# mLSTM denominators: GpSimd adds the scores of the key tiles before the product with ones

## The reference, cut to what matters

```
# per head (4 heads of 128 query/key and 256 value columns), q, k, v over 272 tokens
S    = (q k^T) * exp(D - m_t)          # 272 x 272, causal
num  = S v      + the earlier chunks' part
den  = S.sum(axis=-1) + the earlier chunks' part
h    = num / max(|den|, exp(-m_t))
hm   = rms_norm(h, out_norm_g)
ym   = hm * sigmoid(mo) * silu(mgate)
```

## Time and profile before

| | |
|---|---|
| runs | 1448.88, 1449.24, 1450.42 us |
| profiled execution | 1448.88 us, span 1447.1 us |
| TensorE busy | 1432.7 us (99%) |
| VectorE busy | 1092.7 us (76%) |
| ScalarE busy | 853.7 us (59%) |
| GpSimd busy | 273.1 us (19%) |
| granted clock of TensorE | 0.999 of full speed |

### The profile page before, as it was taken

One profiled execution on the slowest core, in us unless ns is written; L12 is line 12 of the kernel. 1 busy time (PEld: TensorE's weight loads), 2 busy tenths in 40 slices (PEclk: granted clock), 3 DMA queues, 4 the chain that ended last, 5 costly groups with the idle time before them and its releaser, 6 DMA issues.

```text
span 1447.1 us, 27343 instructions
## 1 busy us (share of the span) xinstructions
PE 1432.7 (99%) x9657; PEld 1321.4 (91%) x9657; DVE 1092.7 (76%) x2021; ACT 853.7 (59%) x1559; POOL 273.1 (19%) x329
## 2 busy tenths in 40 slices
PE   8999999999999999999999999999999999999998
PEld 7888899988888888889988888999999999999998
DVE  6777679877756777667787766898778779976883
ACT  6665458766544666446566554656757555576762
POOL 1111113121102111014031113332250035121000
PEclk9999999999999999999999999999999999999999
DMA  6667754556565656565456565554345555434533
GB/s 211 196 196 211 233 180 131 186 179 202 183 188 182 191 187 198 186 195 164 159 171 201 181 188 175 164 145 124 88 127 142 164 153 155 134 94 124 147 118 117
DMA packets 247875, 241.25 MB, mean 167 GB/s; under 512 B 15456, under 2 KB 246736, under 8 KB 247784
## 3 DMA queue, kind: packets, MB, share of 16 engines
q1 hardware_dynamic: 244888, 236.73, 53.8%
q10 hardware_dynamic: 2896, 3.30, 0.8%
HBM read 238.92 MB, written 1.07 MB: 166 GB/s over the span
## 4 chain that ended last, share of the span: by engine, by line
PE 87%; DVE 7%; ACT 3%; issue 2%; DMA 1%; ACTq 0%; SPq 0%; DVEq 0%
PE bank L690 78%; DVE w_lo L1862 2%; DVE work L2458 1%; PE bank L989 1%; ACT w_hi L1124 1%; PE bank L1007 1%; PE bank L972 1%; PE bank L918 1%; DMA raw<-in_w_out_dram 1%; PE bank L928 1%; DVE work L1899 1%; DVE work L2481 1%; DMA raw<-in_ffn_w_in_dram 1%; PE bank L988 1%; ACT L1156 0%
## 5 line engine op out<-in xcount | busy, mean ns | idle before, releaser
L690 PE MATMUL bank<-x_both,w_hi 128*128 128x512 f32 (+2 forms) x3216 | 748.1, 336 | 0.6 <-DVE h L1962 0.5
L1862 DVE TENSOR_TENSOR w_lo<-raw,w_hi 128x1024 fp32r<-128x1024 f32 (+1 forms) x429 | 519.4, 1234 | 203.3 <-ACT w_hi L1124 202.2
L1124 ACT CAST w_hi<-raw 128x1024 fp32r<-128x1024 f32 (+1 forms) x429 | 429.3, 1028 | 125.4 <-PE bank L690 108.3
L690 PEld LDWEIGHTS bank<-x_both,w_hi 128*128 128x128 f32 x3216 | 468.0, 189 | 3.5 <-DVE w_lo L1862 1.1
L690 PEld LDWEIGHTS bank<-x_both,w_lo 128*128 128x128 f32 x2312 | 406.1, 189 | 62.7
L690 PE MATMUL bank<-x_both,w_lo 128*128 128x256 f32 (+1 forms) x2312 | 462.4, 281 | 0.0
L690 PE MATMUL bank<-y_both,w_hi 128*128 128x512 f32 (+2 forms) x1376 | 331.5, 342 | 1.8 <-DVE w_lo L1862 1.1
L690 PEld LDWEIGHTS bank<-y_both,w_lo 128*128 128x128 f32 x1040 | 184.3, 188 | 31.3
L690 PE MATMUL bank<-y_both,w_lo 128*128 128x256 f32 (+1 forms) x1040 | 206.1, 280 | 0.0
L690 PEld LDWEIGHTS bank<-y_both,w_hi 128*128 128x128 f32 x1376 | 200.3, 189 | 2.8 <-DVE w_lo L1862 1.8
L1749 POOL TENSOR_TENSOR work<-work,rstd 128x256 f32<-128x256 f32 x88 | 67.0, 783 | 412.7 <-ACT work L1193 412.7
(11 more groups left out here) (312 smaller groups left out, 1397.9 us busy)
## 6 DMA issues: line engine op xcount, KB each, us to landing
raw<-in_ffn_w_in_dram SPq DMA_DIRECT2D x176, 512.0 KB, 3.8
raw<-in_w_in_dram SPq DMA_DIRECT2D x100, 512.0 KB, 3.7
raw<-in_ffn_w_out_dram SPq DMA_DIRECT2D x64, 512.0 KB, 4.6
raw<-in_w_out_dram SPq DMA_DIRECT2D x32, 512.0 KB, 4.0
raw<-in_ffn_w_out_dram SPq DMA_DIRECT2D x32, 384.0 KB, 3.4
raw<-in_rec_w_in_dram SPq DMA_DIRECT2D x16, 512.0 KB, 4.4
raw<-in_sg_w_in_dram SPq DMA_DIRECT2D x16, 512.0 KB, 4.1
raw<-in_rec_w_out_dram SPq DMA_DIRECT2D x8, 512.0 KB, 3.5
```

Source lines behind the costliest of these rows:

```text
L690: i_ = mm(accs[m][:, cols], w[:, j, m * P:(m + 1) * P], moving, start=begin and g == 0 and not residual, stop=final)
L1124: nc.scalar.copy(hi_part(U)[:, 0:n, :], raw[:, s, 0:n, :]).then_inc(hi_made, 1)
L1862: TT(lo_part(U)[:, 0:n, :], raw[:, s, 0:n, :], hi_part(U)[:, 0:n, :].bitcast(fp32), SUB).then_inc(lo_made, 1)
```

## The change

GpSimd gets a new function, `sums_over_keys`. For each head it adds the second key tile's scores to those of the first in columns 128 to 271, and the third tile's in columns 256 to 271, into `d_sum`, which lies in the place of `v_att`, and raises `d_summed`. TensorE makes the denominators of the queries 0 to 127 from the first tile alone and, after `d_summed`, those of the queries 128 to 271 from `d_sum`.

```
+        d_sum = v_att
...
+        d_summed = sem("d_summed")
...
-                        for t, (a, b) in enumerate(LT):
-                            i_ = mm(bank[4][:, a:L], ones[:, :], m_pt[:, MOFF[t]:MOFF[t] + L - a], start=t == 0, stop=t == 2)
-                        i_.then_inc(m_num, 1)
+                        mm(bank[4][:, 0:P], ones[:, :], m_pt[:, 0:P], start=True, stop=True)
+                        pe.wait_ge(d_summed, n + 1)
+                        mm(bank[4][:, P:L], ones[:, :], d_sum[:, P:L], start=True, stop=True).then_inc(m_num, 1)
...
+                def sums_over_keys():
+
+                    for n in range(M_H * l, M_H * (l + 1)):
+                        pool.wait_ge(m_pt_new, n + 1)
+                        if n % M_H == 0:
+                            pool.wait_ge(kx_mm, l + 1)
+                        else:
+                            pool.wait_ge(m_num, n)
+                        a, b = MOFF[1], MOFF[2]
+                        link(TT(d_sum[:, P:L], m_pt[:, P:L], m_pt[:, a:b], ADD))
+                        TT(d_sum[:, 2 * P:L], d_sum[:, 2 * P:L], m_pt[:, b:MW], ADD).then_inc(d_summed, 1)
+
+                if l:
+                    sums_over_keys()
                 if l == 0:
                     pool.wait_ge(final_r, 1)
                     for c in range(NC8):
                         link(nc.gpsimd.tensor_scalar(h[:, c, META:L], h[:, c, META:L], pcol("final_norm", c), None, MUL))
                         TT(h[:, c, META:L], h[:, c, META:L], sq[:, META:L], MUL).then_inc(h_final, 1)
                     pool.wait_ge(h_final, NC8)
+                    sums_over_keys()
                     h_squares(7, "proj0", 0)
```

## The result

| | before | after |
|---|---|---|
| median | 1449.25 us (18 runs) | 1451.96 us (18 runs) |
| range of the runs | 1448.46 to 1450.42 us | 1449.77 to 1453.96 us |
| profiled execution | 1448.88 us, span 1447.1 | 1453.01 us, span 1451.2 |

The ratio of after to before is 1.0018 (95% interval 1.0012 to 1.0025): 2.7 us slower. The forecast was 1453.2 us. The sign held, and the time lies in the range, but two of the steps that gave it were wrong, and something that I had given 0.06 happened. The median lies 0.1 us under 1452.1 us, where the prediction let slower begin, so by its own bounds the change fell among the outcomes within 0.2%, which had 0.27, and not under slower, which had 0.69. One thing stands out before any trace is opened: the runs after spread over 4.2 us, those before over 2.0.

A forecast was written before the change was run, and what follows sets the result against it. The prediction took the VectorE chain as the bound, with TensorE counting only at head 0 of a layer. To 1448.88 us it added +2.65, +1.05, -0.46 and +1.05, giving 1453.2 us, range 1450.6 to 1455.7 for 8 in 10.

The forecast's parts named there:

- the outcomes within 0.2%: Whole kernel: free additions, no stall at head 0, and the forecast's low end, together 0.27; slower began at 1452.1 us.
- What bounds the kernel: mLSTM: the VectorE chain sets the end, inversions 17.54 us apart; it hangs on TensorE only at head 0 of a layer.
- The wait that is added, layer 0, head 0: TensorE stands 3.0 us for GpSimd's additions, queued behind the final norm; the next unit starts 2.65 us late.
- Layer 1, head 0, denominators shorter: At layer 1's head 0, TensorE's shorter denominators pass their saving to the VectorE chain: -0.46 us.
- What the additions cost VectorE: Heads 1 to 3 of each layer: GpSimd's additions hold VectorE back 0.35 us a head, +1.05 us a layer.
- A small stall there would end ahead of the wait at L1056.: Head 3 of layer 0: additions need 2.1 of 2.4 us; any small stall is covered by an existing wait, costing nothing.
- The clock: Rival: TensorE's clock falls to 1.2 GHz for the unit behind head 0's stall, doubling its 3.09 us: 1456.3 us, chance 0.06.
- The sum: Whole kernel: +2.65, +1.05, -0.46 and +1.05, together +4.3 us on 1448.88, giving 1453.2 us.
- the forecast's own range: Whole kernel, stall and held VectorE: 1451.8 (stall 2.3, 0.15 us a head) to 1455.6 us (3.0, 0.65), chance 0.68.
- What would show it.: Profile signs: 3 us wait at layer 0's head 0, first additions 1.6 us, longer L1056 waits, layer 0 inversions 17.9 us apart.

The follow-up runs named there:

- Two products alone: The kernel before with two denominator products of 128 and 144 columns, no GpSimd additions and no wait for them, denominators incomplete: 1448.25 us, ratio 0.9992.
- the stall filled: The changed kernel with 11 unused products of ones on TensorE ahead of its wait for GpSimd at head 0 of layer 0: 1451.41 us, ratio 1.0018.
- the additions alone: The kernel before, its three products kept, plus GpSimd's additions whose result nobody reads: 1449.10 us, ratio 1.0000.
- the first kernel on GpSimd's kinds: The kernel before with three products plus unread GpSimd instructions, differing by head in size, inputs or operation: 1447.95 us in one run.

## Why the prediction came out, and where its steps failed

- **What bounds the kernel.** Right. The end hangs on the VectorE chain, and only head 0 of a layer passes a change of TensorE on. Two products alone gave 1.1 us less and not 3.7; 3.8 us of waits for GpSimd in later heads cost nothing.
- **"The wait that is added, layer 0, head 0", +2.65 us.** Right. The wait is 2.75 us, the additions 0.49 and 0.22 (taken as 0.50 and 0.25), and with the stall filled the first inversion is later by 2.65.
- **"Layer 1, head 0, denominators shorter", -0.46 us.** Right in kind. From the start of the numerators to the inversion it is 8.67 us where before it was 9.03, so 0.36 of the 0.46 us arrive.
- **"What the additions cost VectorE", 3 x 0.35 us a layer.** Wrong: 0. I took one pair of rows in which GpSimd got in between two splits and carried them to a row of ready VectorE instructions in which it never does. GpSimd lost every turn and paid for it, and I had put the price on VectorE. With the additions alone the ratio is 1.0000. The trace of before has no GpSimd instruction of these kinds that stands longer than 1.9 us, so this row of losses could not be read from it.
- **"A small stall there would end ahead of the wait at L1056."** The place was right, the size was not: with three turns lost and not one, TensorE waits up to 1.25 us at L1054 for GpSimd. As said, it takes the place of the wait at L1056 and costs nothing.
- **The clock.** I had it as a rival with 0.06, because no row that I had read from before has a pause of that length. It fell in all four profiles of the change. The price was too high: I had doubled the whole unit, +3.09 us, and the unit grew by 1.5 us in the first profile; the time grew by 0.6 to 1.2.
- **The sum.** 2.65 for the stall and -0.36 for layer 1 leave +2.3 us, and the stall filled, which is just that, gave +2.1. The forecast added 2.1 us for VectorE, which did not come. The clock put 0.6 to 1.2 us in its place. So 1453.2 is 1.2 us above the median, and what nearness there is comes from a term that was wrong and one that was left out. That 1453.2 lies by the 1453.01 us of the profiled execution is luck twice over, as that one also lost 0.8 us at its start. The bounds of the forecast's own range are misadded: from 1448.88, with the terms given, they come to 1451.6 and 1455.3, not 1451.8 and 1455.6.
- **"What would show it."** The wait of about 3 us came as 2.75. The other signs did not: waits for L1848 take 1.00 to 1.25 us at three later heads, the first addition takes 3.25 us and not 1.6, the L2504 behind it (now L2522) is no longer than before, and the waits at L1056 (now L1059) do not grow but vanish from the list. Of the three signs that the prediction named as proving it wrong, two came: the inversions kept their distance, and the clock fell.

Open stays how the 29 timed runs of the change divide. Seven, at 1449.8 to 1450.6 us, are below all 11 runs with the stall filled (from 1450.94), so a missing fall alone does not explain them, and no profile fell among them. Part of the spread lies in the start of the kernel: the landmark comes between 1039.6 and 1040.6 us in the four profiles. Open is also what let GpSimd in between the two splits of the earlier trace rows: size, kind and moment were tried and don't do it here.

The version with the additions after the sixth chunk has the whole gain of the idea, 1448.06 us. Its slowest run (1448.68) is under the change's fastest (1449.77), measured in another set. Against the kernel before it is 1.3 us ahead by the medians, with an interval that reaches to 1.0000.

## What to carry to other kernels

An engine that is busy 99% need not be the bound. Before work is taken from it, follow the chain through the stage: if another engine's row of work sets the pace, the saving counts only where that row still waits for the busy engine, here at one head of four. Before work is given to an idle engine, ask what stands ahead of it in that engine's program at the first use, and what the engine that can keep it out, here VectorE, is doing at that moment. A wait of TensorE on the chain costs its length (here 2.65 us for a wait of 2.75), and the clock may fall with it (here another 0.6 to 1.2 us of time).

## What the runs showed that was not expected

- VectorE instructions with both inputs in SBUF, the engines' common memory, that follow each other without a gap kept GpSimd out for the whole row: an addition that takes 0.49 us alone took 3.19 to 3.25 us in all 54 such heads of nine profiles of six kernels, and VectorE's instructions in the row took no longer than before. The Trainium skill (SBUF — State Buffer, Who interferes with whom) says that the pair of ports is an exclusive lock for one instruction and goes to whoever issues first. Read as a turn each, that would let the waiting one in after the first split; here VectorE kept the ports over four instructions (the split, L2522 twice, the split).
- A pause of TensorE of 2.75 us came with half the clock for 3.4 or 6.8 us in 4 of 4 profiles, and one of 1.39 us with none. In three of the four the clock fell before the pause had ended. The waits for input at the start of the kernel agree: with one of 2.95 us (the profile after, below) and one of 2.82 us (the first kernel on GpSimd's kinds) the clock is at half for 6.8 us, with one of 2.64 us (the stall filled) it stays at full.

```profile
9.54 1.97 PE L774 MATMUL bank<-con,work 128*128 128x128 f32 x8 [2.95 <-DMA work<-in_x_dram]
```

- 22 records of products with ones, 2.62 us of them in the pause, kept the clock up, and the second product started as late as without them, 31.56 us behind the landmark against 31.55.
